# Transformer layer on one core: where turns and norm steps stand among the attention

## The reference

```python
h = rms_norm(x, norm_pre_mix)
proj = h @ w_in                                   # q, k, v, indexer, HGRN2 parts
att_out = dsa_attention(q, k, v, qi, ki, wi)      # 8 heads of 64; per query the 256 keys
                                                  # with the highest indexer score
hg_out = hgrn2_mixer(hq, hf, hi, hg, ...)         # gated linear recurrence, 4 heads
x = x + rms_norm(concat(att_out, hg_out) @ w_out, norm_post_mix)
h2 = rms_norm(x, norm_pre_ffn)
ff = (silu(h2 @ w_gate) * (h2 @ w_up)) @ w_down   # width 2816
x = x + rms_norm(ff, norm_post_ffn)
```

## Time and profile before

| | |
|---|---|
| median of 3 runs | 3596.58 us (3594.59 to 3598.08) |
| profiled execution | 3594.16 us, span 3592.4 us |
| mean granted clock of TensorE | 0.945 |
| TensorE busy | 3306.7 us (92%) |
| VectorE busy | 2320.6 us (65%) |
| ScalarE busy | 1509.5 us (42%) |
| GpSimd busy | 239.5 us (7%) |
| memory traffic | 94 GB/s over the span |

### The profile page before, as it was taken

One profiled execution on the slowest core, in us unless ns is written; L12 is line 12 of the kernel. 1 busy time (PEld: TensorE's weight loads), 2 busy tenths in 40 slices (PEclk: granted clock), 3 DMA queues, 4 the chain that ended last, 5 costly groups with the idle time before them and its releaser, 6 DMA issues. The chain is left out here.

```text
span 3592.4 us, 46162 instructions
## 1 busy us (share of the span) xinstructions
PE 3306.7 (92%) x17984; PEld 2903.6 (81%) x17984; DVE 2320.6 (65%) x3705; ACT 1509.5 (42%) x2429; POOL 239.5 (7%) x413
## 2 busy tenths in 40 slices
PE   8999999988667799999888999998899999979998
PEld 8999999888646688888667888887788888768886
DVE  3466676777567666676777677777867765443445
ACT  3343544444354444343454444444544443333222
POOL 0000000000111100000110101000200000010000
PEclk9999999999866899999889999998999999989999
DMA  4424343322201322222422222123211212342233
GB/s 176 158 103 149 115 143 123 111 106 105 78 22 39 106 82 81 71 82 76 158 77 67 77 66 77 65 87 123 87 63 56 73 61 68 105 144 97 91 103 108
DMA packets 139770, 339.48 MB, mean 94 GB/s; under 512 B 14368, under 2 KB 35360, under 8 KB 132384
## 3 DMA queue, kind: packets, MB, share of 16 engines
q1 hardware_dynamic: 137248, 332.32, 27.0%
q10 hardware_dynamic: 2304, 4.20, 0.3%
HBM read 283.44 MB, written 53.02 MB: 94 GB/s over the span
## 5 line engine op out<-in xcount | busy, mean ns | idle before, releaser
L1849 PE MATMUL PJ_d<-h_hi,wd_hi 128*128 128x512 f32 x1408 | 560.4, 398 | 12.4 <-DVE h_lo L1638 12.4
L1851 PE MATMUL PJ_d<-h_hi,wd_lo 128*128 128x512 f32 x1408 | 551.6, 392 | 0.0
L1850 PE MATMUL PJ_d<-h_lo,wd_hi 128*128 128x512 f32 x1408 | 550.7, 391 | 0.0
L1392 ACT ACTIVATE wd_hi<-wd_raw 128x512 fp32r<-128x512 f32 x592 | 359.6, 627 | 275.7 <-DMA wd_raw<-in_w_gu 170.4
L1633 DVE TENSOR_TENSOR wd_lo<-wd_raw,wd_hi 128x512 fp32r<-128x512 f32 x592 | 396.6, 690 | 54.6 <-ACT wd_hi L1392 52.0
L657 PE MATMUL PJ<-w_hi,h_hi 128*128 128x342 f32 (+1 forms) x1280 | 418.4, 327 | 4.2 <-DVE w_lo L490 4.2
L659 PE MATMUL PJ<-w_hi,h_lo 128*128 128x342 f32 (+1 forms) x1280 | 411.3, 321 | 0.0
L658 PE MATMUL PJ<-w_lo,h_hi 128*128 128x342 f32 (+1 forms) x1280 | 411.2, 321 | 0.0
L1617 DVE CUSTOM_DVE_ANT_0 prob<-SA,bias 128x1024 f32<-128x1024 f32 (+7 forms) x192 | 170.3, 912 | 365.2 <-PE SA L1776 364.8
L1387 ACT ACTIVATE pT<-SA 128x512 f32<-128x512 f32 (+3 forms) x320 | 156.6, 531 | 569.2 <-PE SA L1802 569.2
L1814 PEld LDWEIGHTS SC<-V,pT 128*128 128x128 f32 x2176 | 293.3, 207 | 49.4 <-ACT pT L1387 38.1
(11 more groups left out here) (186 smaller groups left out, 5879.7 us busy)
## 6 DMA issues: line engine op xcount, KB each, us to landing
wd_raw<-in_w_gu SPq DMA_DIRECT2D x352, 256.0 KB, 3.0
wd_raw<-in_w_down SPq DMA_DIRECT2D x176, 256.0 KB, 2.6
w_raw<-in_w_in SPq DMA_DIRECT2D x20, 1368.0 KB, 6.1
w_raw<-in_w_in SPq DMA_DIRECT2D x20, 1352.0 KB, 6.1
row_h<-proj_d SPq DMA_DIRECT2D x16, 1024.0 KB, 8.4
wd_raw<-in_w_out SPq DMA_DIRECT2D x64, 256.0 KB, 3.8
proj_d<-stage SPq DMA_DIRECT2D x40, 342.0 KB, 5.4
proj_d<-stage SPq DMA_DIRECT2D x40, 338.0 KB, 3.8
```

The lines of the kernel that those rows point to most:

```text
L1392: s_.activation(w_hi[:, u % RING, :], w_raw[:, u % RING, :], ACT.Copy).then_inc(w_hi_ready, 1)
L1849: t.matmul(to, w_hi[:, r, w], h_hi[:, c, :], start=(c == 0), stop=False)
L1850: t.matmul(to, w_hi[:, r, w], h_lo[:, c, :], start=False, stop=False)
L1851: last = t.matmul(to, w_lo[:, r, w], h_hi[:, c, :], start=False, stop=(c == KD - 1))
```

## The change

The planner counts the steps apart. A turn takes 3.0 of attention's weight and a gap step 4.5 for itself; what is left of the weight is shared equally by the pieces. Before, a turn or gap step had as much beside it as any piece. Further, in the last superblock the first three `out` pieces go before turn 3, and the first three turns (`EARLY`) are dealt out over the slots too, so they lie in block 15. SyncE's load of the last tile of `mix_d` then stands right behind the store of block 15's output. In a step VectorE now makes the low half of a turn first, then the norm, then the two residual additions.

```diff
--- before.py
+++ after.py
@@ -775,8 +775,9 @@
 
     items = []
     for s in range(NS):
-        items += [("turn", s, i) for i in range(TS)]
-        items += [("out", s, kg, n, i) for kg in range(2) for n in range(2) for i in range(TS)]
+        turns = [("turn", s, i) for i in range(TS)]
+        outs = [("out", s, kg, n, i) for kg in range(2) for n in range(2) for i in range(TS)]
+        items += turns + outs if s + 1 < NS else turns[:3] + outs[:3] + turns[3:] + outs[3:]
         items += [("gap", s, k) for k in range(6)]
         made = 0
         for g, (f0, f1) in enumerate(GROUPS):
@@ -862,22 +863,26 @@
             for name, share in zip("ABC", shares):
                 slot((name, b, h), head * share)
 
+    EARLY = 3
+    BESIDE = {"turn": 3.0, "gap": 4.5}
     fills, done = {}, 0
     for s in range(NS - 1):
         def first_slot(b):
             return slots.index(("s", b))
         window = slots[first_slot(TS * (s + 1)):(first_slot(TS * (s + 2)) if s + 2 < NS else len(slots))]
-        mine = [n for n, x in enumerate(items) if x[1] == s]
-        total_w, total_c = sum(weight[k] for k in window), len(mine)
+        last = at["turn", s + 1, 0] - 1 if s + 2 < NS else at["turn", s + 1, EARLY - 1]
+        mine = [x[0] for x in items[done:last + 1]]
+        beside = sum(BESIDE.get(x, 0) for x in mine)
+        each = (sum(weight[k] for k in window) - beside) / sum(x not in BESIDE for x in mine)
         so_far, spent = 0.0, 0.0
         for k in window:
             so_far += weight[k]
             first = done
-            while done <= mine[-1] and spent + 1 <= total_c * so_far / total_w + 1e-6:
-                spent += 1
+            while done <= last and spent + BESIDE.get(items[done][0], each) <= so_far + 1e-6:
+                spent += BESIDE.get(items[done][0], each)
                 done += 1
             fills[k] = (first, done)
-        assert done == mine[-1] + 1
+        assert done == last + 1
 
     with ExitStack() as ctx:
         def sb(name, shape, dt=F32):
@@ -1029,7 +1034,7 @@
                         pt_order[b, h, c] = len(pt_order)
                     enter(("pT", b, h, p), "pt")
                     enter_slot(("BC"[p], b, h))
-        TAIL = (at["turn", NS - 1, 0], len(items))
+        TAIL = (done, len(items))
         enter_items(*TAIL)
 
         def pair(key):
@@ -1183,7 +1188,8 @@
                         load_back(s - 1, 3)
                 if x == ("turn", s, 1):
                     wait_pair_full(sp, ("mT", s, 1))
-                    load_mix(s, 3)
+                    if s + 1 < NS:
+                        load_mix(s, 3)
                     if s:
                         store_out(s - 1, 1)
                 if x == ("turn", s, 2):
@@ -1248,6 +1254,7 @@
                     for name in "ABC"[0:1 + pairs_of(b)]:
                         fill((name, b, h))
             store(NB - 1)
+            load_mix(NS - 1, 3)
             for n in range(*TAIL):
                 after(n)
             store_out(NS - 1, 0)
@@ -1699,16 +1706,16 @@
                     hidden(y)
                 if z[0] == "up" and z[3:] == (0, 1):
                     gate(z)
-                if last_out(n - 3):
-                    add_mix(item_at(n - 3)[1], item_at(n - 3)[4])
-                if last_out(n - 5):
-                    norm_x1(item_at(n - 5)[1], item_at(n - 5)[4])
-                if last_down(n - 3):
-                    finish(item_at(n - 3)[1], item_at(n - 3)[4])
                 if x[0] == "turn":
                     turned_low(("mT", x[1], x[2]), x[2])
                 if x[0] == "gap" and x[2] >= 2:
                     turned_low(("hT", x[1], x[2] - 2), x[2] - 2)
+                if last_out(n - 5):
+                    norm_x1(item_at(n - 5)[1], item_at(n - 5)[4])
+                if last_out(n - 3):
+                    add_mix(item_at(n - 3)[1], item_at(n - 3)[4])
+                if last_down(n - 3):
+                    finish(item_at(n - 3)[1], item_at(n - 3)[4])
                 for u in splits_at.get(n - 1, []):
                     split_unit(u)
```

## The result

The changed kernel takes 3642.58 us (median of 4 runs, 3641.67 to 3649.61) against 3595.94 us: a ratio of 1.0135, 95% interval 1.0123 to 1.0148. It is slower by 47 us, where +17 us were forecast, and outside the range. The profiled execution is the longest of the four, 3649.6 us with a span of 3647.8 us, 55 us over that of before; so single stretches of its trace show some 7 us more in all than its median. Its mean granted clock is 0.936, that of the other three 0.942 or 0.943.

A forecast was written before the change was run, and what follows sets the result against it. The prediction took VectorE's own work, more than latency, to bound the turn and norm stretches. Its four parts, 15 - 3 + 9 - 4 = +17 us, gave 3613 us, with a range of 3574 to 3634 us.

The forecast's parts named there:

- What bounds the kernel: Six turn and norm stretches lose 122 us: 25 us with VectorE idle, 97 us VectorE's own work, not latency.
- The low half ahead of the residual work: VectorE's new order within a step: shortens one wait and lengthens another, costed at nothing.
- Part 2, superblock 1: Steps in blocks 8 and 9: attention keeps VectorE's surplus, some latency goes; -3 us, from -10 to +2.
- Part 3, superblock 2: Steps in blocks 12 and 13: norm steps move to where VectorE's work is above the mean; +9 us, 0 to +13.
- Part 1, superblock 0: Steps among blocks 4 and 5: ten nearly bare heads, loss scaled from block 3; +15 us, from -5 to +22.
- Part 4, the last superblock: Three turns in block 15, three pieces before turn 3: 10.3 us of waits go, others come; -4 us, -9 to +2.
- The sum: Whole kernel: 15 - 3 + 9 - 4 = +17 us, so 3613 us; bounds add to -24 and +39.
- Latency after all: Rival for the whole kernel: waits are latency, so it gets faster, 3563 us, half of that 3580; chance 0.32.
- The tail decides: Rival: late last scaling delays block 15's store; 4 to 6 us more, up to 3634; 0.06 together with stuck queue.
- No change: Rival: VectorE's surplus is the same wherever it lies; 3597 us, -7 to +7; chance 0.17.
- It doesn't do what it says: Rival: a step still waits in a queue, last head stalls 3 to 8 us; 0.06 together with the tail rival.
- The rule on the clock: Stretches with bare attention: by this rule alone all run near half clock, putting the sum at its upper end.

The follow-up runs named there:

- b3: Kernel before without VectorE's eight own halvings per block and the loop for more than 8 left keys: 3582.84 us.
- c2: Kernel before with only the turns spaced (3.0 of attention's weight each; norm steps as before): 3595.90 us, ratio 1.0005.
- c1: Kernel before with only the norm steps spaced (4.5 of attention's weight each; turns like pieces): 3628.72 us, ratio 1.0097.
- a3: Kernel before with only the spacing (3.0 and 4.5 beside turns and norm steps of superblocks 0 to 2): 3628.51 us, ratio 1.0093.
- a4: Changed kernel with the old order within a VectorE step: 3625.05 us, ratio 1.0080 against the kernel before.
- c3: Kernel before with only 0.4 of attention's weight beside each turn and norm step: 3568.94 us, ratio 0.9927.
- e1: Kernel before with turns and norm steps back to back, no attention beside them: -27.4 us, ratio 0.9924.

## Why the prediction was wrong

- **What bounds the kernel.** Right in the direction: of the 122 us lost in six stretches only 25 had VectorE idle, attention beside the steps does not pay, and the table of amounts beside a norm step bears that out from both sides. That the other 97 us are VectorE's own work was argued and is not shown: b3 takes 80 us of VectorE's busy time out of blocks 8 to 11 and 73 us out of blocks 12 to 15, and the whole kernel becomes 11.9 us faster.
- **The low half ahead of the residual work: "shortens one wait and lengthens another: nothing".** This is the step that failed most. It costs 17 us in the changed kernel and 28 us alone. I had looked at who gets the result earlier, not at what VectorE can do while it waits: of a step's inputs, the low half's is the one that is being made just then.
- **Part 2, superblock 1: -3 us.** Measured +12.6 in the kernel with the spacing alone. I had given the 9.6 us of VectorE's idle time back and put the half clock at 2 us, although part 1 had the row for it (0.57 in block 3). Busy time grew by 13.2 us with the same instructions.
- **Part 3, superblock 2: +9 us.** Measured +20.9 with the spacing alone. That it would be idle time of TensorE was right (18.5 of 20.9 us), the size was half. One term had the wrong sign: I took the turns at -2 us, and c2, with the turns spaced alone, is 10.7 us longer there. c1 has +22.6 us, so the two do not add. Which work in these heads makes the rest stays open; taking the halvings out removes 5 us of the idle time.
- **Part 1, superblock 0: +15 us.** Measured +2.8 us with the spacing alone, no more than the spread of this part, and +7.9 in the changed kernel's profile. The turns' part is even a gain there: with c2's turns blocks 4 to 7 take 588.1 us, 9.6 less. Scaling block 3's rate was wrong for these heads: the granted clock is 0.79 in the first stretch and 0.67 in the second, not 0.5 to 0.6, and the 9.53 us wait behind GpSimd's reduction went, as forecast.
- **Part 4, the last superblock: -4 us.** Right: -3.5 us between a3 and a4, the waits 1.6, 1.70 and 2.46 us where 2, 2 and 2.46 were reckoned. In other orders it costs 3 to 6 us, more than the +2 that its range allowed.
- **The sum.** 33.3 - 3.5 + 17 = 47 us. Parts 1 to 3 together were forecast at 21 and are 33. That they come so near is partly luck: by a3's trace one is 12 us too high and the two others 16 and 12 us too low. The rest of the miss is the step order; a4, without it, is at 3625.05 us, inside the range.
- **The rivals.** *Latency after all* is out: the clock is under 0.85 in each of the six stretches, and with the steps pushed together (c3) the kernel is faster. *The tail decides*: its condition was a scaling more than 6 us after the last value matmul; it comes at 3194.02, 3.8 us after the end of the matmuls at 3190.2. *No change* is out by the result. *It doesn't do what it says* had a stuck queue, and turn 0 of the last superblock shows no wait above 1 us.
- **The rule on the clock** in TensorE: Matmul & The Clock Gate (the Trainium skill, HAM oscillation), by which pauses between bursts let the clock fall again and again, would have put the sum at its upper end. The trace agrees in part: the clock is 0.68 and 0.62 in the new stretches of blocks 8 and 9, where it was 0.75 and 0.70, but 0.78 and 0.76 in those of blocks 12 and 13, and none is near half clock throughout.

## What to carry to other kernels

Before spacing steps out to hide a wait, ask whether the engine that is waited for idles in it, and whether what is put between loads it less than it loads the waiting engine; where not, try to push the steps together and keep the filler for places that have none. Where an engine goes through its instructions in the written order, as VectorE here, an instruction whose input is just being made goes last in its step. When a part of a change is costed at nothing, it still needs a bound; here an exchange of six lines was a third of the loss.

## What the runs showed that was not expected

Bare attention of the same instructions costs by the clock as much as by waits: in a3, TensorE's idle time in blocks 8 to 11 did not change (40.8 and 40.3 us) while its busy time rose from 639.4 to 652.5 us. And no attention at all beside turns and norm steps is 27 us faster than an even spread. The norm steps of e1, in the view by windows, for superblocks 0 and 1 (the third, from 2505 us, is like them):

```profile
1233.00:1250.00 17.00, 8.94 (x37) 7.34 (x37) 15.39 (x15) 8.94 (x14) 5.05 (x7) 0.52 0.29 109
1836.00:1853.00 17.00, 8.93 (x38) 7.73 (x39) 15.40 (x15) 8.81 (x14) 6.13 (x8) 0.50 0.34 125
```

TensorE is busy for 8.9 of 17 us at half clock, and that is cheap all the same: VectorE is busy for 15.4 us of each, so the steps pass nearly as fast as its own work allows, and the clock is low for 17 us only. With attention between them the same steps take 68 to 76 us, at a mean clock of 0.62 to 0.76.
